# Seven block products in place of eight for the down projections of a feed-forward, with ScalarE and VectorE staggered by a step

## Chip, core and metric

The kernel runs on one core of a Trainium2 chip. Its engines are TensorE (PE: matmuls from SBUF into eight PSUM banks of 512 fp32 columns), VectorE (DVE), ScalarE (ACT), GpSimd (POOL) and SyncE (SP), which here only issues transfers. The metric is the device time of one execution in microseconds (us); lower is better.

## What is computed

Two blocks follow each other on 256 tokens of width 1024. The first has two layers of three kinds of attention, each with a gated feed-forward; the second has a mixer of four branches and a feed-forward with a squared ReLU. The change concerns only that last feed-forward:

```python
u = rms_norm(h, norm_mlp_pre[l])
hid = jnp.square(jax.nn.relu(jnp.einsum("btd,df->btf", u, w_up[l])))    # 1024 -> 4096
m = jnp.einsum("btf,fd->btd", hid, w_down[l])                           # 4096 -> 1024
h = h + rms_norm(m, norm_mlp_post[l])
```

All of it is fp32. The kernel gets the accuracy from two roundings: each operand is split into a high part, rounded to the type that TensorE multiplies in one pass, and a low part, the rest. A product is the sum of three matmuls: high by high, high by low, low by high.

## The kernel before

**Weights.** They come as a stream of tiles of 128 partitions by 2048 fp32 columns (1 MB), in the order of `stream_plan` (for the feed-forward: up 0, up 1, down 0, up 2, down 1, and so on). `load` (L2845 on) brings a tile into one of four `raw` slots as soon as the tile four places back has been split. ScalarE writes the high part (`whi`, L1374), then VectorE (L1895) or, for some tiles, GpSimd (L2772, in pieces of 256 columns) writes `wlo = raw - whi`. `whi` and `wlo` have three slots each (`SPL`). Each engine's program is written in order, and `ahead(...)` places the split of the tile two ahead into it. In the feed-forward of the second block both splits belong to ScalarE and VectorE; GpSimd has none.

**The feed-forward.** It runs in 16 steps. Step j computes 256 hidden features: `wide` (L735) makes two blocks of 128 features by 512 columns (256 tokens times the high and the low part of the input) in banks 0 and 1 or 2 and 3, with 8 matmuls of 512 columns each and 8 of 256 for the low part of the weights. VectorE adds the two halves of each block with a reduction that reads PSUM (`summed`, L1931) and squares the positive part in place (L2727) into `cc` or `th`; ScalarE rounds it to `gh` (L1868), and VectorE writes `gl` (L2729). `down` (L756) of step j-1 then adds 2 token halves x 2 feature blocks x 2 column halves, each three matmuls of 512 columns (L771 to L773), into the four banks 4 to 7, where they stay until the last step. `down_quarter` (L776) does the last step one bank at a time, so that the norm can begin on the first.

**Around it.** Before the stage stands the norm `post1`: ScalarE squares and sums, VectorE adds, GpSimd takes the root (`root`, L2781), VectorE multiplies by the gain and adds to the residual stream `X` (L2379, L2387), and TensorE transposes `X` (L586) for the up projection. After it stands the same with `post2`, and four transfers out.

```python
for j in range(16):                                   # tensor_program, second block
    b = 2 * (j % 2)
    if j:
        wide(tile_at[2, "up", j, 0], (b, b + 1), lp)
...
    if j:
        down(tile_at[2, "down", j - 1, 0], j - 1, False)
```

## Time and profile before

| | us |
|---|---|
| median of 3 runs | 1020.5 |
| lowest, highest | 1020.02, 1020.83 |
| span of the profiled execution | 1018.8 |

| engine | busy us | share of the span |
|---|---|---|
| TensorE | 1010.3 | 99% |
| VectorE | 758.5 | 74% |
| ScalarE | 556.8 | 55% |
| GpSimd | 232.6 | 23% |

The span is the profiled execution's own time between its first and last instruction; the runs' times include what lies around it. The stage of the change is the last sixth of the span. Matmuls overlap in the array, so the length of a single one is not its share of TensorE's time; the difference of two starts is.

### The profile page before, as it was taken

What the parts mean: (1) busy time and instruction counts of PE and PEld (TensorE: products, weight loads), DVE (VectorE), ACT (ScalarE), POOL (GpSimd) and SP (SyncE); (2) the same over time, 40 slices, a digit from 0 to 9 for tenths busy, and PEclk for the clock granted to TensorE, in tenths of its full rate; (3) what the DMA queues carried; (4) which work ended last, traced back from release to release, by engine and by line L of the source; (5) the groups of instructions that cost most, each with busy time, mean ns of one, the idle gap of its engine ahead of it and who ended that gap; (6) DMA issues with size and microseconds to landing.
All of it is one profiled execution on the core that took longest, in us unless ns stands there. A gap on an engine that the chain in (4) does not pass through costs nothing.

```text
span 1018.8 us, 14751 instructions
## 1 busy us (share of the span) xinstructions
PE 1010.3 (99%) x5688; PEld 851.1 (84%) x5688; DVE 758.5 (74%) x1208; ACT 556.8 (55%) x848; POOL 232.6 (23%) x322
## 2 busy tenths in 40 slices
PE   9999999999999999999999999999999999999997
PEld 6877788888888877788888888998888888888886
DVE  6997568788777887578787778888865457766665
ACT  6575566545556466656554556845544455334433
POOL 0572600000000272800000004019947620000000
PEclk9999999999999999999999999999999999999999
DMA  9641545555554351365554544553445556564541
GB/s 362 232 159 59 176 155 207 190 182 207 194 180 173 114 218 42 125 221 193 212 195 177 207 168 163 171 201 119 170 150 184 204 186 227 191 214 174 182 149 41
DMA packets 27894, 180.24 MB, mean 177 GB/s; under 512 B 3120, under 2 KB 3248, under 8 KB 7472
## 3 DMA queue, kind: packets, MB, share of 16 engines
q1 hardware_dynamic: 27824, 179.30, 49.5%
q8 instruction: 45, 0.74, 0.3%
q14 instruction: 25, 0.20, 0.1%
HBM read 178.24 MB, written 1.05 MB: 176 GB/s over the span
## 4 chain that ended last, share of the span: by engine, by line
PE 97%; DVE 1%; ACT 1%; DMA 0%; issue 0%; SPq 0%; DVEq 0%
PE pb L747 17%; PE pb L752 10%; PE pb L609 9%; PE pb L610 9%; PE pb L612 8%; PE pb L772 6%; PE pb L771 6%; PE pb L773 6%; PE pb L754 3%; PE pb L1017 2%; PE pb L970 2%; PE pb L673 1%; PE pb L672 1%; PE pb L674 1%; PE pb L709 1%; PE pb L985 1%
## 5 line engine op out<-in xcount | busy, mean ns | idle before, releaser
L1895 DVE TENSOR_TENSOR wlo<-raw,whi 128x2048 fp32r<-128x2048 f32 (+1 forms) x125 | 282.8, 2265 | 102.4 <-ACT whi L1374 102.2
L1374 ACT ACTIVATE whi<-raw 128x2048 fp32r<-128x2048 f32 x159 | 298.5, 1881 | 60.5 <-PE pb L612 34.6
L2772 POOL TENSOR_TENSOR wlo<-raw,whi 128x256 fp32r<-128x256 f32 x268 | 206.8, 810 | 318.9 <-ACT whi L1374 315.2
L747 PE MATMUL pb<-hb,whi 128*128 128x512 f32 x770 | 183.7, 389 | 0.0
L747 PEld LDWEIGHTS pb<-hb,whi 128*128 128x128 f32 x770 | 144.6, 188 | 30.4
L609 PE MATMUL pb<-whi,hb 128*128 128x512 f32 x336 | 134.2, 399 | 0.1
L610 PE MATMUL pb<-wlo,hb 128*128 128x512 f32 x336 | 130.9, 390 | 0.0
L612 PE MATMUL pb<-whi,hb 128*128 128x512 f32 x320 | 124.9, 390 | 0.0
L752 PEld LDWEIGHTS pb<-hb,wlo 128*128 128x128 f32 x880 | 112.8, 191 | 4.3
L752 PE MATMUL pb<-hb,wlo 128*128 128x256 f32 x880 | 114.2, 283 | 0.0
L772 PE MATMUL pb<-wlo,gh 128*128 128x512 f32 x280 | 109.2, 390 | 0.0
L773 PE MATMUL pb<-whi,gl 128*128 128x512 f32 x280 | 109.1, 390 | 0.0
L771 PE MATMUL pb<-whi,gh 128*128 128x512 f32 x280 | 109.0, 389 | 0.0
L2781 POOL TENSOR_TENSOR sm<-sm 128x1 f32<-128x1 f32 x12 | 6.5, 553 | 422.7 <-DVE sm L1903 243.3
L609 PEld LDWEIGHTS pb<-whi,hb 128*128 128x128 f32 x336 | 63.1, 188 | 14.5 <-issue 2.3
L610 PEld LDWEIGHTS pb<-wlo,hb 128*128 128x128 f32 x336 | 63.2, 188 | 12.1
L612 PEld LDWEIGHTS pb<-whi,hb 128*128 128x128 f32 x320 | 60.1, 188 | 12.8
L771 PEld LDWEIGHTS pb<-whi,gh 128*128 128x128 f32 x280 | 52.6, 188 | 11.6 <-issue 0.3
L772 PEld LDWEIGHTS pb<-wlo,gh 128*128 128x128 f32 x280 | 52.6, 188 | 11.2
L773 PEld LDWEIGHTS pb<-whi,gl 128*128 128x128 f32 x280 | 52.6, 188 | 11.0
L1538 ACT ACTIVATE gh<-th 128x512 fp32r<-128x512 f32 x22 | 13.9, 632 | 76.3 <-DVE th L2281 76.3
L754 PE MATMUL pb<-hb,whi 128*128 128x512 f32 x110 | 34.7, 397 | 0.0
(404 smaller groups left out, 1558.8 us busy)
## 6 DMA issues: line engine op xcount, KB each, us to landing
raw<-wst SPq DMA_DIRECT2D x159, 1024.0 KB, 4.8
raw<-wst SPq DMA_DIRECT2D x10, 512.0 KB, 4.3
gb<-gains SPq DMA_DIRECT2D x3, 512.0 KB, 6.4
XN<-xt SPq DMA_DIRECT2D x2, 512.0 KB, 5.3
X<-x SPq DMA_DIRECT2D x1, 1024.0 KB, 12.1
out<-X SPq DMA_DIRECT2D x4, 256.0 KB, 2.0
PQ<-prm SPq DMA_DIRECT2D x1, 909.0 KB, 4.5
raw<-wst SPq DMA_DIRECT2D x2, 256.0 KB, 7.3
```

The lines of the kernel that those rows point to most:

```text
L609: e.matmul(o, high[:, s], wh[:, k, :], start=first and k == 0, stop=False)
L610: mm = e.matmul(o, high[:, s], wl[:, k, :], start=False, stop=False)
L612: mm = e.matmul(o, low[:, s], wh[:, k, :], start=False, stop=last and k == 3)
L747: e.matmul(b[:, :], wh[:, k, s], hb2[:, k, :, :].rearrange("p i q -> p (i q)"), start=k == 0, stop=False)
L752: e.matmul(b[:, 0:L], wl[:, k, s], hh[:, k, :], start=False, stop=False)
L754: mm = e.matmul(b[:, :], wh[:, 7, s], hb2[:, 7, :, :].rearrange("p i q -> p (i q)"), start=False, stop=True)
L771: e.matmul(o, ah, wh[:, k, c], start=j == 0 and k == 0, stop=False)
L772: e.matmul(o, ah, wl[:, k, c], start=False, stop=False)
L773: mm = e.matmul(o, al, wh[:, k, c], start=False, stop=last and k == 1)
L1374: e.activation(whi[:, split_slot(m), 0:w], raw[:, m % RAW, 0:w], ACT.Copy).then_inc(*hi(m))
L1895: e.tensor_tensor(wlo[:, split_slot(m), s], raw[:, m % RAW, s], whi[:, split_slot(m), s].bitcast(F32), ALU.subtract).then_inc(*lo_v(m))
L2772: g = e.tensor_tensor(wlo[:, split_slot(m), s], raw[:, m % RAW, s], whi[:, split_slot(m), s].bitcast(F32), ALU.subtract)
```

## The change

Each step's down product is a product of 2 x 2 blocks: hidden features in two blocks by tokens in two halves (the first operand), features by column halves (the weights). The changed kernel forms it as seven block products in place of eight, in the form that uses sums of blocks: products 1, 2 and 4 take blocks of hidden features as they are, products 3, 5, 6 and 7 take sums of such blocks over the token halves (token sums); the weights are the four quarters of the down tile, one of them rewritten as a sum, and three more sums of quarters (weight sums). Each of the seven accumulates over the 16 steps in a PSUM bank of its own (banks 1 to 7), and the four blocks of the result are put together from them once, at the end. Bank 0 alone is left for the up blocks.

- **TensorE**: `wide_block` makes one up block; the products of a step are spread over two places, 3, 5, 6, 7 of step j-2 between the two up blocks of step j and 1, 2, 4 of step j-1 behind them.
- **ScalarE** copies each up block from PSUM into `E` (`evict`), rounds the token sums and the weight sums as well (`features_high`, `sums_high`), and is a step behind with `gh`.
- **VectorE** adds the halves out of `E`, forms three token sums, and writes the low halves of `gh`, of the token sums and of two of the three weight sums.
- **GpSimd** forms the three weight sums and one sum in the raw tile itself (`weight_sums`, pieces of 256 columns) and the low half of the third weight sum (`sums_low`).
- The weights of a down tile are laid out in memory as four blocks of 512 columns. The split of a down tile waits for `weight_sums`, since that changes the raw tile. Odd down tiles have their own slot (`odd_high`, `odd_low`), in memory that earlier stages used.
- At the end ScalarE copies product 1, VectorE makes four totals with seven additions, and the gain of the first column half goes to GpSimd; the second token half goes out first.

The core of the diff:

```diff
+            def quarter_products(j, *names):
+                m = downs[j]
...
+                for n in names:
+                    if n in (1, 2, 4):
+                        weights_ready(m)
+                        q.wait_ge(*gl_done[m])
+                    else:
+                        q.wait_ge(*tokens_lo[j])
+                    if n in (5, 6):
+                        q.wait_ge(*sums_lo[j])
+                    if n == 7:
+                        q.wait_ge(*sums_lo_g[j])
...
+                    e.matmul(o, high, w_high, start=j == 0, stop=False)
+                    e.matmul(o, high, w_low, start=False, stop=False)
+                    mm = e.matmul(o, low, w_high, start=False, stop=j == 15)
...
-                for j in range(16):
-                    b = 2 * (j % 2)
-                    if j:
-                        wide(tile_at[2, "up", j, 0], (b, b + 1), lp)
...
+                for j in range(1, 16):
+                    wide_block(ups[j], 0, up_bank(j, 0), lp)
+                    free[up_bank(j, 0)] = ff_low[2, j, 0]
+                    if j > 1:
+                        quarter_products(j - 2, 3, 5, 6, 7)
+                    wide_block(ups[j], 1, up_bank(j, 1), lp)
+                    free[up_bank(j, 1)] = ff_low[2, j, 1]
+                    quarter_products(j - 1, 1, 2, 4)
+                quarter_products(14, 3, 5, 6, 7)
+                quarter_products(15, 1, 2, 4, 6, 7, 5, 3)
...
+                for j in range(16):
+                    if j > 1:
+                        quarters_high(j - 1)
+                    evict(j, 0)
                     if j:
-                        ahead(2, "down", j - 1, 0)
...
+                        features_high(j - 1)
+                    if j == 15:
+                        quarters_high(15)
+                    if j:
+                        sums_high(j - 1)
+                    evict(j, 1)
+                    if j < 14:
+                        split(ups[j + 2])
...
+                pieces(o[:, 0:512], r[:, 1024:1536], r[:, 0:512], ALU.subtract).then_inc(*pool())
+                pieces(o[:, 1024:1536], r[:, 1536:2048], r[:, 1024:1536], ALU.add)
+                q.wait_ge(*q.prev)
+                pieces(o[:, 512:1024], r[:, 1536:2048], o[:, 0:512], ALU.add).then_inc(*pool())
+                q.wait_ge(*q.prev)
+                pieces(r[:, 1024:1536], o[:, 512:1024], r[:, 512:1024], ALU.subtract).then_inc(*summed_w(j))
...
+            q.wait_ge(*b_used[3, 1, 1, "sum"])
+            weight_sums(0)
             root("post1")
-            m = ahead_to(m, 2, "down", 15, 0)
-            root("post2")
+            for j in range(16):
+                if j < 15:
+                    weight_sums(j + 1)
...
+                sums_low(j)
+            for t in range(2):
+                post_gain(t)
+            root("post2", (1, 0))
```

**VectorE, one step near the end.** Before, the low halves of down tile 13 and up tile 15, then step 14 up to `gl`; `[waits ...]` names the signals that an instruction waits for (`hi`: the high half is written; `used`, `half_used`: TensorE is through with a tile or its first block).

```order
L1895 TENSOR_TENSOR wlo<-raw,whi 128x2048 [waits hi]
L1895 TENSOR_TENSOR wlo<-raw,whi 128x2048 [waits used,hi]
L1931 TENSOR_REDUCE cc<-pb 128x256 [waits half_used]
L1931 TENSOR_REDUCE cc<-pb 128x256 [waits used]
L2727 SCALAR_TENSOR_TENSOR cc<-cc 128x512 [waits ff_sum]
L2729 TENSOR_TENSOR gl<-cc,gh 128x512 [waits gh_done]
```

After, the low halves of up tile 15 and down tile 13, `gl` and the sums' low halves of step 13, then the hidden features and token sums of step 14 (`shared_low` and `odd_low` are low halves of the weight sums and of odd down tiles, `tokens_low` and `mg` low halves of token sums):

```order
L2042 TENSOR_TENSOR wlo<-raw,whi 128x2048 [waits used,hi]
L2042 TENSOR_TENSOR odd_low<-raw,odd_high 128x2048 [waits hi]
L2897 TENSOR_TENSOR gl<-th,gh 128x512 [waits gh_done]
L2900 TENSOR_TENSOR mg<-token_sums,mg 128x512 [waits tokens_hi]
L2871 TENSOR_TENSOR shared_low<-sums_51,shared_high 128x1024 [waits sums_hi]
L2880 TENSOR_TENSOR cc<-E 128x512 [waits ff_low]
L2882 SCALAR_TENSOR_TENSOR cc<-cc 128x512 [waits ff_sum]
L2888 TENSOR_TENSOR token_sums<-cc 128x256 [waits ff_glu,tokens_lo]
L2890 TENSOR_TENSOR token_sums<-token_sums,cc 128x128 [waits dve]
L2892 TENSOR_TENSOR token_sums<-token_sums,cc 128x128 [waits dve]
```

Two reductions out of PSUM have become an addition out of `E`, and four kinds of operations are new; `gl` of a step no longer follows its own hidden features but stands behind both splits of the next round.

**GpSimd, from the last low half ahead of the feed-forward.** Before:

```order
L2772 TENSOR_TENSOR wlo<-raw,whi 128x256 [waits used,hi]
L2772 TENSOR_TENSOR wlo<-raw,whi 128x256 x7
L2825 MEMSET PT 128x512 [waits mm_small]
L2781 TENSOR_TENSOR sm<-sm 128x1 [waits mean_sq] x4
```

After, to the sums of down tile 1 (`sums` are the weight sums, `sm` the norm's statistics, from which `root` takes its powers):

```order
L3076 MEMSET PT 128x512 [waits mm_small]
L3002 TENSOR_TENSOR sums_50<-raw 128x256 [waits s_raw3,b_used]
L3002 TENSOR_TENSOR sums_50<-raw 128x256 x3
L3002 TENSOR_TENSOR sums_50<-raw,sums_50 128x256 [waits pool]
L3002 TENSOR_TENSOR sums_50<-raw,sums_50 128x256
L3002 TENSOR_TENSOR raw<-sums_50,raw 128x256 [waits pool]
L3002 TENSOR_TENSOR raw<-sums_50,raw 128x256
L3032 TENSOR_TENSOR sm<-sm 128x1 [waits mean_sq] x2
L3002 TENSOR_TENSOR sums_51<-raw 128x256 [waits s_raw1]
L3002 TENSOR_TENSOR sums_51<-raw 128x256 x3
L3002 TENSOR_TENSOR sums_51<-raw,sums_51 128x256 [waits pool]
L3002 TENSOR_TENSOR sums_51<-raw,sums_51 128x256
```

The sums of the first down tile stand ahead of the norm's root now, and eight pieces for each further tile behind it, with two for a low half in each step.

**TensorE, the last up tile and the start of the products behind it.** Before:

```order
L747 MATMUL pb<-hb,whi 128x512 [waits ff_sum]
L747 MATMUL pb<-hb,whi 128x512 x6
L752 MATMUL pb<-hb,wlo 128x256 [waits lo_v]
L752 MATMUL pb<-hb,wlo 128x256 x15
L754 MATMUL pb<-hb,whi 128x512 x2
L771 MATMUL pb<-whi,gh 128x512 [waits gl_done,lo_v,hi]
L772 MATMUL pb<-wlo,gh 128x512
L773 MATMUL pb<-whi,gl 128x512
L771 MATMUL pb<-whi,gh 128x512
L772 MATMUL pb<-wlo,gh 128x512
```

After, from product 7 of step 13 over the second block of up tile 15 to product 1 of step 14:

```order
L859 MATMUL pb<-shared_high,mg 128x512 [waits sums_lo_g]
L860 MATMUL pb<-shared_low,mg 128x512
L861 MATMUL pb<-shared_high,mg 128x512
L819 MATMUL pb<-hb,whi 128x512 [waits ff_low]
L819 MATMUL pb<-hb,whi 128x512 x6
L823 MATMUL pb<-hb,wlo 128x256 x8
L824 MATMUL pb<-hb,whi 128x512
L859 MATMUL pb<-whi,gh 128x512 [waits gl_done,lo_v,hi]
L860 MATMUL pb<-wlo,gh 128x512
L861 MATMUL pb<-whi,gl 128x512
```

The second block's matmuls begin when the copy of the first has left bank 0 (`ff_low`), and behind them come products 1, 2 and 4 of the step before.

## Rows read from the trace of the kernel before

**Rows 1.** Page, part 1, whole span: busy us (share) x instructions.
```profile
PE 1010.3 (99%) x5688; PEld 851.1 (84%) x5688; DVE 758.5 (74%) x1208; ACT 556.8 (55%) x848; POOL 232.6 (23%) x322
```

**Rows 2.** Chain of waits: start us, us, engine, output, line, count.
```profile
975.06 3.17 PE pb L747 x14
978.24 1.91 PE pb L752 x16
980.15 0.47 PE pb L754 x2
986.07 3.17 PE pb L747 x14
...
997.08 3.17 PE pb L747 x14
```

**Rows 3.** VectorE's timeline, one step: start, us, operation, count [idle before].
```profile
929.91 2.29 DVE L1895 TENSOR_TENSOR wlo<-raw,whi 128x2048 fp32r<-128x2048 f32 x1 [1.11 <-ACT whi L1374]
...
936.39 1.29 DVE L1931 TENSOR_REDUCE th<-pb 128x256 f32<-128x512 f32 x2 [1.01 <-PE pb L754]
937.72 0.69 DVE L2727 SCALAR_TENSOR_TENSOR th<-th 128x512 f32<-128x512 f32 x1
```

**Rows 4.** ScalarE's timeline in the same step.
```profile
931.13 1.92 ACT L1374 ACTIVATE whi<-raw 128x2048 fp32r<-128x2048 f32 x1 [1.26 <-PE pb L773]
938.44 0.63 ACT L1868 ACTIVATE gh<-th 128x512 fp32r<-128x512 f32 x1 [5.39 <-DVE th L2727]
```

**Rows 5.** GpSimd's timeline, with the count of pieces.
```profile
347.26 5.84 POOL L2772 TENSOR_TENSOR wlo<-raw,whi 128x256 fp32r<-128x256 f32 x8 [24.95 <-ACT whi L1374]
...
797.16 3.94 POOL L2772 TENSOR_TENSOR wlo<-raw,whi 128x256 fp32r<-128x256 f32 x4 [1.69 <-ACT whi L1374]
803.49 5.61 POOL L2772 TENSOR_TENSOR wlo<-raw,whi 128x256 fp32r<-128x256 f32 x8 [2.40 <-ACT whi L1374]
812.63 7.04 POOL L2772 TENSOR_TENSOR wlo<-raw,whi 128x256 fp32r<-128x256 f32 x8 [3.52 <-ACT whi L1374]
...
831.48 0.56 POOL L2781 TENSOR_TENSOR sm<-sm 128x1 f32<-128x1 f32 x1 [11.35 <-DVE sm L1903]
...
1011.86 0.55 POOL L2781 TENSOR_TENSOR sm<-sm 128x1 f32<-128x1 f32 x1 [177.11 <-DVE sm L2738]
```

**Rows 6.** VectorE's timeline ahead of the second block's output projection.
```profile
798.59 1.21 DVE L2694 TENSOR_TENSOR PQ<-PQ 128x512 f32<-128x512 f32 x1
799.72 0.67 DVE L2688 SCALAR_TENSOR_TENSOR PQ<-PQ,pb 128x512 f32<-128x512 f32 x1
...
809.93 0.69 DVE L2694 TENSOR_TENSOR PQ<-PQ 128x512 f32<-128x512 f32 x1
...
811.90 2.29 DVE L1895 TENSOR_TENSOR wlo<-raw,whi 128x2048 fp32r<-128x2048 f32 x1
```

**Rows 7.** VectorE's timeline in the first block's second layer.
```profile
347.00 0.29 DVE L2011 TENSOR_TENSOR sc<-sc,mskt 128x128 f32<-128x128 f32 x1
...
349.44 0.83 DVE L542 TENSOR_TENSOR sm<-PQ,prmt 128x128 f32<-128x128 f32 x1
350.19 0.82 DVE L543 TENSOR_TENSOR sm<-PQ,prmt 128x128 f32<-128x128 f32 x1
```

**Rows 8.** Weight load issued at 819.7: duration ns, starts; then issue to landing.
```profile
L2852 SPq DMA_DIRECT2D raw<-wst x1: 328/328/328, 819.7 to 819.7; - x1
...
DMA to landing us min/median/max: 8.1/8.1/8.1
```

**Rows 9.** Who waited for whom from 819 to 850: total us, times, longest.
```profile
PEld pb L586 <- DVE X L2387: 0.7, 2, 0.5
```

**Rows 10.** VectorE's timeline, its last operations.
```profile
1015.35 1.41 DVE L2387 SCALAR_TENSOR_TENSOR X<-XN,sm,X 128x512 f32<-128x512 f32 x2
```

**Rows 11.** VectorE's low halves, all: duration ns min/median/max.
```profile
L1895 DVE TENSOR_TENSOR wlo<-raw,whi x125: 1237/2292/2295, 22.6 to 999.1; 128x2048 fp32r<-128x2048 f32 x122, 128x1024 fp32r<-128x1024 f32 x3
```

**Rows 12.** Stretch after the last matmul: busy us by engine, then granted TensorE clock.
```profile
1014.00:1018.80 4.80, 0.00 (x0) 0.00 (x0) 2.65 (x5) 0.25 (x2) 0.55 (x1) 0.65 0.58 219
```

More of the change, by code:

```diff
@@ L388, in stacked @@
             return whi[:, split_slot(m), 0:1024].rearrange("p (k i c) -> p k i c", k=8, i=2)
+        ups = [tile_at[2, "up", j, 0] for j in range(16)]
+        downs = [tile_at[2, "down", j, 0] for j in range(16)]
+        last_out = tile_at[2, "out", 1, 1]
+        ODD_SLOT = 3
         def split_slot(m):
+            if m in ups:
+                return nth[ups[ups.index(m) % 2]] % SPL
+            if m == downs[15]:
+                return split_slot(ups[14])
+            if m in downs:
+                return ODD_SLOT if downs.index(m) % 2 else nth[last_out] % SPL
             return nth[m] % SPL
         def slot_before(m):
+            if m in ups[2:]:
+                return ups[ups.index(m) - 2]
+            if m == downs[15]:
+                return ups[14]
+            if m in downs:
+                return downs[downs.index(m) - 2] if downs.index(m) > 1 else last_out
             return order[nth[m] - SPL] if nth[m] >= SPL else None
@@ L755, in wide, with wide_block @@
                     mm.then_inc(*(used(m) if j else half_used(m)))
+            def wide_block(m, i, bank, ready):
+                wh, wl = (w.rearrange("p (k c) -> p k c", k=8) for w in parts(m))
+                s, b = slice(128 * i, 128 * i + 128), PB[bank]
+                q.wait_ge(*hi[m])
+                bank_free(bank)
+                for k in range(7):
+                    q.wait_ge(*ready[k])
+                    e.matmul(b[:, :], wh[:, k, s], hb2[:, k, :, :].rearrange("p i q -> p (i q)"), start=k == 0, stop=False)
+                q.wait_ge(*ready[7])
+                q.wait_ge(*lo_of(m)[m])
+                for k in range(8):
+                    e.matmul(b[:, 0:L], wl[:, k, s], hh[:, k, :], start=False, stop=False)
+                mm = e.matmul(b[:, :], wh[:, 7, s], hb2[:, 7, :, :].rearrange("p i q -> p (i q)"), start=False, stop=True)
+                mm.then_inc(*(used(m) if i else half_used(m)))
@@ L1858, in second_block, with evict @@
                 high_half(n, 1, par2("lp"))
-                for j in range(16):
-                    ahead(2, "up", j, 0)
-                    if j == 0:
-                        square_half(n, 0)
-                        square_half(n, 1)
-                    z = (cc, th)[j % 2][:, :, :]
+                def evict(j, i):
+                    q.wait_ge(*(used if i or not j else half_used)[ups[j]])
+                    if j > 1:
+                        q.wait_ge(*ff_sum[2, j - 2])
+                    elif j:
+                        q.wait_ge(*squares[("lp", 2), 1, 1])
+                    e.activation(E[:, 2 * (j % 2) + i, :], PB[up_bank(j, i)][:, :], ACT.Copy).then_inc(*ff_low(2, j, i))
@@ new lines, in second_block @@
+                sums_high(15)
+                features_high(15)
+                q.wait_ge(*product[1])
+                q.wait_ge(*ff_sum[2, 15])
+                e.activation(E[:, 0, :], PB[PRODUCTB[1]][:, :], ACT.Copy).then_inc(*act("first product"))
+                for i, (t, c) in enumerate(((0, 0), (1, 0), (1, 1), (0, 1))):
+                    q.wait_ge(*total[t, c])
+                    e.activation((E[:, 2, :], E[:, 3, :], rl[:, 0, :], rl[:, 1, :])[i], total_at[t, c], ACT.Square, scale=1.0 / 32,
+                                 accum_out=norm_of["post2"][:, 2 * t + c:2 * t + c + 1]).then_inc(*squares("post2", t, c))
@@ L2713, in second_block @@
+                split(downs[0])
                 for j in range(16):
[L2714 removed]
                     if j == 1:
[L2716 to L2721 removed]
@@ L2730, in second_block @@
-                    if j:
-                        ahead(2, "down", j - 1, 0)
-                ahead(2, "down", 15, 0)
-                for t in range(2):
-                    post_gain("post2", t, 0, 48)
-                    q.wait_ge(*squares["post2", t, 1])
+                        input_scale()
+                    if 0 < j < 15:
+                        split(ups[j + 1])
+                    if j > 1:
+                        split(downs[j - 1])
+                    if j:
+                        features_low(j - 1)
@@ new lines, in second_block @@
+                    if j == 15:
+                        q.wait_ge(*hi[downs[15]])
+                        high, low = parts(downs[15])
+                        e.tensor_tensor(low[:, 0:1024], raw[:, downs[15] % RAW, 0:1024], high[:, 0:1024].bitcast(F32),
+                                        ALU.subtract).then_inc(*lo_v(downs[15]))
+                    if j:
+                        sums_low(j - 1)
+                    hidden_and_sums(j)
+                features_low(15)
+                sums_low(15)
@@ new lines, in second_block, with bank @@
+                one, up, upper, side = E[:, 0, :], sums_at[0][:, 512:1024], sums_at[0][:, 1024:1536], E[:, 1, :]
+                def bank(i):
+                    q.wait_ge(*product[i])
+                    return PB[PRODUCTB[i]][:, :]
+                q.wait_ge(*act["first product"])
+                e.tensor_tensor(total_at[0, 0], one, bank(2), ALU.add).then_inc(*total(0, 0))
+                e.tensor_tensor(up, one, bank(6), ALU.add).then_inc(*dve())
+                q.wait_ge(*q.prev)
+                e.tensor_tensor(upper, up, bank(7), ALU.subtract).then_inc(*dve())
@@ L2881, in sync_program @@
                 load(m)
-            for t in range(2):
+            for t in (1, 0):
                 for n in range(2):
```

220 lines of the change are left out of this document (175 added, 45 removed).

## The prediction

> **What bounds the kernel now.** I read the page's busy shares first, then the chain of waits through the stage of the change, then VectorE's, ScalarE's and GpSimd's timelines there. TensorE is busy for 99% of the span [rows 1], and in the stage of the change the chain is TensorE alone. One of the sixteen steps takes 986.07 - 975.06 = 11.0 us: 5.55 us for two up blocks (3.17 + 1.91 + 0.47) and 5.46 us for the 24 matmuls of a down tile, 0.2275 us each [rows 2]. The 0.39 us that a matmul has in other views is its length in the pipeline, not its share of time. In such a step VectorE works on the two low halves (2.29 each), 1.29 on the two PSUM reductions and 0.69 each on the squaring and gl, about 7.2 us with idle stretches between [rows 3]; ScalarE works 1.92 us on each of two high halves and 0.63 on gh, 4.4 us together [rows 4]; GpSimd does nothing for 177 us before 1011.86 [rows 5]. So anything taken from TensorE counts, until another engine needs more than TensorE does.
>
> **What TensorE saves.** Seven products of three matmuls replace eight: 21 for 24. That is 3 x 0.2275 = 0.68 us a step, 10.9 us over 16 steps, and the step that TensorE asks for is 10.33 us. Nothing else on TensorE changes in size.
>
> **What the others get.** What counts is the distance from one start to the next: a row's length less 0.09 us where operations are independent (two reductions of 0.69 take 1.29), and plus 0.03 where the next waits for it [rows 3]. That gives 2.19 us for 2048 columns, 0.60 or 0.72 for 512, and by the slope between them 1.12 for 1024, 0.45 for 256 and 0.32 or 0.20 for 128.
> ScalarE adds per step two evictions (0.60 each), one more 512-column rounding and 1536 columns of rounded sums (about 1.4): 4.4 + 3.3 = 7.7 us. It fits into 10.33.
> VectorE keeps the two low halves (4.38), does gl and the new low half of the token sums (1.20), 1024 columns of the sums' low halves (1.12), the addition out of E and the squaring (1.44), and three token sums (0.98): 9.1 us in ten operations. Alone it would fit too, with 1.2 us to spare.
> GpSimd gets ten pieces of 256 columns per step, eight for the weight sums and two for a low half, at 0.70 us a piece when nothing disturbs it (5.61 for eight) [rows 5]: 7.0 us. Alone it fits.
>
> **But VectorE and GpSimd don't run alone.** The same 512-column addition of two SBUF operands (L2694) takes 0.69 us while GpSimd is idle (809.93) and 1.21 us while GpSimd works (798.59, between pieces that began at 797.16) [rows 5, 6]: it waits 0.53 us for a piece to end. Operations in a row on 128 columns, 0.29 us with GpSimd idle (347.00), come out at 0.83 us while eight pieces run (347.26), and their pitch of 0.75 us is 0.13 us of columns plus 0.62 for a piece [rows 5, 7]. The other way round, eight pieces that begin inside a 2048-column subtraction take 7.04 us instead of 5.61; the extra 1.4 us is what was left of that subtraction (811.90 + 2.29 = 814.19) [rows 5, 6]. L2688, which has one operand in PSUM, keeps its 0.67 us beside the pieces [rows 6]. So the two engines exclude each other when both VectorE operands lie in SBUF, whichever is first.
> Today that is harmless: GpSimd is idle in this stage, and each reduction reads PSUM. After the change all ten VectorE operations have two SBUF operands (the up results come through E now), and GpSimd always has pieces waiting. The two take turns: 9.1 us plus ten waits of 0.53, less 0.1 us in each of the dependent ones, where the piece starts in the gap that was there anyway, is 14.0 to 14.4 us. By the port's own time: 7680 columns at 1.04 ns (2.29 - 0.69 us for 1536 columns) are 8.0 us, ten pieces at 0.62 are 6.2, together 14.2. I take **14.2 us a step**. Who has priority doesn't matter to this sum. TensorE, at 10.33, waits some 3.8 us in each step for gl of the tile before its products 1, 2 and 4.
> The Trainium skill weighs in here: its page "SBUF — State Buffer", section "Who interferes with whom", says that a VectorE instruction with two SBUF inputs and a GpSimd instruction that reads SBUF contend for a port pair, and that whoever is first holds it for the whole instruction. The rows agree on the exclusion (1.21 against 0.69 us). They show a little less than the whole instruction, since by that reading a step would be 9.1 + 7.0 = 16.1 us and the total about 1103 us; that is a rival below.
>
> **The edges.** Here I went through the five engines' lists in their new order by hand, each operation starting when its engine, its signals and, on VectorE and GpSimd, the shared port are free, with the durations above and weight loads landing in time, as they do now. GpSimd now does the weight sums of tile 0 ahead of the root for the norm in front of the stage. Tile 0 is issued at 819.7 and lands 8.1 us later, at 827.8 [rows 8]; eight pieces and two waits between them end at 833.6, and the root ran at 831.48 [rows 5]. That is 2.1 us late, on the path, since TensorE already waits for the residual updates behind it, 0.7 us in all [rows 9]. The second token half's updates and the low half of up tile 1 meet pieces of tile 1's sums, 3 x 0.53. Together +3.7 us before up tile 1.
> Steps 1 and 2: GpSimd still idles between its jobs, TensorE has no or few products to do, and by the same count the two take 22.1 us against 22.0: +0.1.
> Steps 3 to 14: 12 x (14.2 - 11.0) = +38.
> The end, from the start of up tile 15 to the last residual update: before, 997.08 to 1016.76, 19.7 us [rows 2, 10]. After, VectorE begins step 14's addition 0.6 us later, needs 15.6 us to step 15's (no up tile to split, but 3.4 us of waiting for ScalarE, which waits for GpSimd's last sums), 8.6 us for that step and its low halves, and 8.8 us for seven combinations (0.6 or 0.72 each), the gains, the root (0.55) and four updates (0.6 each): 33.6 us, +13.9.
> The gain of 10.9 us is inside these step times, not added. Sum: 3.7 + 0.1 + 38 + 13.9 = +55.7. The profiled span is 1018.8 us, and its run's time is 1.7 us more than the span, as the median of 1020.5 has it: 1020.5 + 55.7 = **1076 us**.
>
> **Bounds of the unknown.** No low half of 2048 columns in the trace ever began behind a piece (the longest of all took 2.295 us) [rows 11], so its wait is not shown. At zero for both of them a step is 13.1 us and the total 1076 - 14 x 1.1 = 1061; at a whole pitch of 0.70 us for all ten it is 15.0 and 1087. I take 0.53 since all 128 to 512-column cases agree on it.
>
> **Rivals.** (1) *The exclusion bites one way only*: VectorE waits for about half of its operations, and a waiting piece still slips through. 9.1 + 5 x 0.53 = 11.8 us a step, 14 x 2.4 less: 1043. Against it: the 7.04 us [rows 5]. (2) *No exclusion here*, as if these tiles didn't meet: TensorE sets the pace. -10.9, +3.7 at the start, +2.1 of waits for gl in the first and last step, +2.4 for the longer combination behind the last matmul (the four additions that depend on each other, then the gains): -2.7, 1018 us. This is the case on the other side; it decides if VectorE's step stays below 10.33 us, for which its ten waits together would have to stay below 1.2 us. (3) *Whole instructions exclude*, 16.1 us a step: 1103. (4) *TensorE's clock falls in the new gaps.* After TensorE's last matmul the granted clock of the last 4.8 us averages 0.65 [rows 12], so with TensorE idle it fell to the lower level, 1.2 GHz, and the new waits leave TensorE idle too. At half clock the 10.33 us of a step stretch into the wait that is there anyway; only if nearly all of it ran so would a step be 20.7 us and the total near 1165. A slower TensorE also removes the gap that slows it, so I expect a lower clock on the page and no more time. The Trainium skill, page "TensorE: Matmul & The Clock Gate", section "Why this matters for your kernels", warns of idle gaps between bursts of matmuls for this reason; the row agrees as to the direction.
>
> **Chances.** Forecast, 1061 to 1087: 0.72. (1) 0.10, (2) 0.07, (3) 0.07, (4) 0.04. The range takes in the forecast's bounds and (1): 1042 to 1090. Three runs of this kernel tell about 0.2%, 2 us, from no change; (2) lies just beyond that, so of its 0.07 I count 0.04 as faster and 0.03 as same. All the rest is slower, 0.93.
>
> **What would show it.** Right: TensorE 10 or 12 points less busy in the second block's last stretch, its waits put down to VectorE's gl or the low halves; VectorE near 100% there, 512-column operations at 1.2 us and 2048-column ones at 2.8; GpSimd pieces whose mean is well above 0.7; steps of 14.2 us. Wrong: 512-column operations at 0.69 us beside working GpSimd, or steps of 10.3 us. The start is wrong if the root's operation of the norm ahead of the stage still starts by 831.5 us.

## The result, and the profile after

The changed kernel takes **1076.0 us** (median of 4 runs, 1075.6 to 1078.4) against 1020.5 us before (4 runs, 1020.0 to 1020.8): a ratio of 1.055, 95% interval 1.054 to 1.057. It is 55.6 us slower. The span of the profiled execution grew from 1018.8 to 1074.5 us, by 55.7.

The page of the changed kernel, part 1 (busy us, share, instructions), the slices of TensorE and of its granted clock, and the chain's shares by engine:
```profile
PE 1022.6 (95%) x5638; PEld 855.0 (80%) x5640; DVE 862.9 (80%) x1277; ACT 605.8 (56%) x913; POOL 446.1 (42%) x490
...
PE   9999999999999999999999999999999887888794
...
PEclk9999999999999999999999999999999898998987
...
PE 75%; DVE 15%; POOL 3%; issue 3%; DMA 2%; ACT 1%; SPq 0%; DVEq 0%; POOLq 0%; ACTq 0%
```
Against [rows 1], TensorE went from 99% to 95% of a longer span although its program has 48 matmuls fewer (the count of weight loads; of the matmul records two more are missing), VectorE did 104 us more, and GpSimd's busy time nearly doubled. TensorE's slices fall from 9 to 8 and 7 exactly where the stage of the change begins. Its busy time rises, since a matmul counts longer when it runs at the lower clock.

VectorE's timeline for one step (start us, us, engine, line, operation, count), where [rows 3] show the step before:
```profile
927.01 0.77 DVE L2888 TENSOR_TENSOR token_sums<-cc 128x256 f32<-128x256 f32 x1
927.81 0.71 DVE L2890 TENSOR_TENSOR token_sums<-token_sums,cc 128x128 f32<-128x128 f32 x1
928.56 0.71 DVE L2892 TENSOR_TENSOR token_sums<-token_sums,cc 128x128 f32<-128x128 f32 x1
929.20 5.56 DVE L2042 TENSOR_TENSOR wlo<-raw,whi 128x2048 fp32r<-128x2048 f32 x2
934.68 1.21 DVE L2897 TENSOR_TENSOR gl<-cc,gh 128x512 fp32r<-128x512 f32 x1
...
938.62 1.22 DVE L2880 TENSOR_TENSOR th<-E 128x512 f32<-128x512 f32 x1
...
941.20 0.78 DVE L2888 TENSOR_TENSOR token_sums<-th 128x256 f32<-128x256 f32 x1
```
From one L2888 to the next are 14.19 us, with no idle time in a bracket. The 512-column operations take 1.21 us, not 0.69, and the two of 2048 columns 5.56, not the 4.48 that two take undisturbed (shown below). GpSimd's timeline in the same step:
```profile
925.54 3.58 POOL L3002 TENSOR_TENSOR sums<-raw 128x256 f32<-128x256 f32 x4 [0.33 <-DMA raw<-wst]
929.08 3.52 POOL L3002 TENSOR_TENSOR sums<-raw,sums 128x256 f32<-128x256 f32 x2
932.68 3.79 POOL L3002 TENSOR_TENSOR raw<-sums,raw 128x256 f32<-128x256 f32 x2
936.43 2.86 POOL L3016 TENSOR_TENSOR shared_low<-sums,shared_high 128x256 fp32r<-128x256 f32 x2
939.82 1.87 POOL L3002 TENSOR_TENSOR sums<-raw 128x256 f32<-128x256 f32 x2 [0.53 <-DMA raw<-wst]
```
Ten pieces last 13.75 us, 1.4 us each, twice the 0.70 us of a piece alone [rows 5]. Both engines are full, and each spends a good part of that time waiting for the other: about half of it on GpSimd, about a third on VectorE. What TensorE waited for between 850 and 1060 us (waiter, releaser: total us, times, longest):
```profile
PE pb L859 <- DVE gl L2897: 35.9, 14, 3.7
PE pb L859 <- DVE shared_low L2871: 2.6, 1, 2.6
```
So it waits for `gl` in 14 places, 2.6 us in the mean; the rest of what a step has too much goes into matmuls at the lower clock.

### The profile page after: what moved, and what is told of

It reads as the page before. It is cut to its first block, busy times and chain, and to the rows that moved or that the text cites. A ratio compares the mean times of both kernels' runs of the same rounds, so it can differ in the third digit from the quotient of the medians.

```text
span 1074.5 us, 14968 instructions
## 1 busy us (share of the span) xinstructions
PE 1022.6 (95%) x5638; PEld 855.0 (80%) x5640; DVE 862.9 (80%) x1277; ACT 605.8 (56%) x913; POOL 446.1 (42%) x490
## 4 chain that ended last, share of the span: by engine, by line
PE 75%; DVE 15%; POOL 3%; issue 3%; DMA 2%; ACT 1%; SPq 0%; DVEq 0%; POOLq 0%; ACTq 0%
PE pb L801 12%; PE pb L663 8%; PE pb L664 7%; PE pb L666 7%; PE pb L806 7%; DVE wlo L2042 4%; PE pb L882 3%; PE pb L883 3%; PE pb L881 3%; PE pb L808 2%; POOL sums L3002 2%; PE pb L1127 2%; PE pb L1080 2%; DVE shared_low L2871 2%; DMA raw<-wst 2%
## 5 line engine op out<-in xcount | busy, mean ns | idle before, releaser
L1485 ACT ACTIVATE whi<-raw 128x2048 fp32r<-128x2048 f32 x143 | 268.0, 1878 | 43.8 <-PE pb L666 34.6
L801 PE MATMUL pb<-hb,whi 128*128 128x512 f32 x560 | 133.7, 389 | 0.0
L801 PEld LDWEIGHTS pb<-hb,whi 128*128 128x128 f32 x560 | 105.1, 188 | 22.2
L806 PEld LDWEIGHTS pb<-hb,wlo 128*128 128x128 f32 x640 | 82.1, 191 | 3.1
L806 PE MATMUL pb<-hb,wlo 128*128 128x256 f32 x640 | 83.0, 283 | 0.0
L882 PE MATMUL pb<-wlo,gh 128*128 128x512 f32 x160 | 62.4, 390 | 0.0
L883 PE MATMUL pb<-whi,gl 128*128 128x512 f32 x160 | 62.3, 389 | 0.0
L881 PE MATMUL pb<-whi,gh 128*128 128x512 f32 x160 | 62.3, 389 | 0.0
L3002 POOL TENSOR_TENSOR sums<-raw 128x256 f32<-128x256 f32 x64 | 56.5, 911 | 13.8 <-DMA raw<-wst 11.8
L819 PE MATMUL pb<-hb,whi 128*128 128x512 f32 x210 | 57.4, 416 | 0.0
L1649 ACT ACTIVATE gh<-th 128x512 fp32r<-128x512 f32 x22 | 13.9, 632 | 76.3 <-DVE th L2427 76.3
L3002 POOL TENSOR_TENSOR raw<-sums,raw 128x256 f32<-128x256 f32 x32 | 54.4, 1719 | 1.3
## 6 DMA issues: line engine op xcount, KB each, us to landing
X<-x SPq DMA_DIRECT2D x1, 1024.0 KB, 12.2
```

What stands on the lines that cost most here:

```text
L801: e.matmul(b[:, :], wh[:, k, s], hb2[:, k, :, :].rearrange("p i q -> p (i q)"), start=k == 0, stop=False)
L806: e.matmul(b[:, 0:L], wl[:, k, s], hh[:, k, :], start=False, stop=False)
L881: e.matmul(o, ah, wh[:, k, c], start=j == 0 and k == 0, stop=False)
L882: e.matmul(o, ah, wl[:, k, c], start=False, stop=False)
L883: mm = e.matmul(o, al, wh[:, k, c], start=False, stop=last and k == 1)
L1485: e.activation(parts(m)[0][:, 0:w], raw[:, m % RAW, 0:w], ACT.Copy).then_inc(*hi(m))
```

## The experiments

Times are medians, but for two kernels that ran once, where the text says so. Each experiment was run beside the kernel before on the same chip, and ratios are against it. "A step" is the mean distance of the hidden addition (L2880) from step 1 to step 15, if nothing else is said.

**Take the reads away, keep everything else.** Rival (2) and the forecast differ only in whether GpSimd's pieces disturb VectorE. So the pieces become writes without a source.
```diff
-                        g = e.tensor_tensor(dst[:, c:c + PIECE], a[:, c:c + PIECE], b[:, c:c + PIECE], op)
+                        g = e.memset(dst[:, c:c + PIECE], 0.0)
```


> GpSimd's ten pieces per step in the feed-forward are replaced by memsets of the same columns: it writes and signals as before but reads nothing, so the weight sums are wrong and the output isn't the reference's. Nothing else differs from the changed kernel. Theory (VectorE and GpSimd exclude each other when both read SBUF with two operands on VectorE): VectorE's 512-column operations go back from 1.22 to 0.69 us and the 2048-column ones from 2.83 to 2.29, a step is TensorE's 10.3 us, and the total is 1015 to 1021 us. Rival (VectorE's or ScalarE's amount of work sets the pace whatever GpSimd does): 1060 us or more. Rival (half of the waits come from elsewhere): about 1043 us.

Measured: 1017.1 us, ratio 0.997 (0.996 to 0.998), a step of 10.4 us. VectorE's timeline, then a row of GpSimd's:
```profile
925.77 0.69 DVE L2880 TENSOR_TENSOR cc<-E 128x512 f32<-128x512 f32 x1 [0.72 <-ACT E L1977]
...
928.29 4.48 DVE L2042 TENSOR_TENSOR wlo<-raw,whi 128x2048 fp32r<-128x2048 f32 x2
...
936.12 0.69 DVE L2880 TENSOR_TENSOR th<-E 128x512 f32<-128x512 f32 x1 [0.73 <-ACT E L1977]
```
```profile
927.43 1.58 POOL L3002 MEMSET sums<- 128x256 f32 x6 [3.01 <-DMA raw<-wst]
```
The same operations are back at 0.69 and 4.48 us, VectorE idles again, and the step is what TensorE asks for (10.33 by the prediction). So nothing but the pieces makes the change slow. The writes are also shorter (0.26 us each), but that isn't what helps: in the steps of the changed kernel VectorE never stands idle, so what decides is how long its own operations take. The run also bounds the idea: if the sums cost VectorE nothing, the whole gain would be 3 us.

**Fewer pieces.** The second piece of each pair in the weight sums, four a step, becomes such a write.
```diff
+                        if c:
+                            g = e.memset(dst[:, c:c + PIECE], 0.0)
+                        else:
+                            g = e.tensor_tensor(dst[:, c:c + PIECE], a[:, c:c + PIECE], b[:, c:c + PIECE], op)
```

> Every second piece of the weight sums is a memset, so four of the ten pieces per step read nothing; half of the sums' columns are wrong and the output isn't the reference's. Theory: the step is the sum of what both engines hold, 8.0 us of VectorE columns and 0.62 us for each reading piece: 8.0 + 6 x 0.62 = 11.7 us, 2.5 us less in each of some 14 steps, so about 1041 us (1036 to 1047). Rival (a threshold: any contention costs all of it): stays near 1076 us. Rival (GpSimd's own chain of work sets the pace, its pieces being slow): the memsets are shorter than pieces but still count, about 1055 us.

Measured: 1046.5 us in a single run, just inside the range, and a step of 12.2 us where 11.7 were expected. Six pieces give 12.20 and ten give 14.16: 0.49 us a piece, close to the 0.53 us that one wait takes.

**No pieces, their work on VectorE.** The weight sums and the whole low half of the sums (1536 columns) are VectorE's:
```diff
+                    e.tensor_tensor(o[:, 0:512], r[:, 1024:1536], r[:, 0:512], ALU.subtract).then_inc(*dve())
+                    e.tensor_tensor(o[:, 1024:1536], r[:, 1536:2048], r[:, 1024:1536], ALU.add)
...
+                    if 0 < j < 15:
+                        weight_sums(j + 1)
                     hidden_and_sums(j)
```


> VectorE does all of GpSimd's feed-forward pieces itself: four additions of 512 columns per step and 1536 columns of the sums' low half in place of 1024; GpSimd does nothing in the stage but its last tile's part and the roots. Same results, same other engines. Theory: nobody to wait for, VectorE needs 9.1 + 2.6 + 0.5 = 12.2 us a step, 2.0 us less than together with GpSimd, total about 1047 us (1040 to 1054), although VectorE has more work than in the changed kernel. Rival (VectorE is simply overloaded, its operations long for a reason of their own): 14.2 + 3.2 = 17.4 us a step, near 1120 us.

Measured: 1078.9 us in a single run, a miss by 32 us. VectorE's waits (850 to 1060) and its timeline:
```profile
DVE sums L2878 <- DMA raw<-wst: 24.5, 12, 2.2
```
```profile
932.09 0.69 DVE L2878 TENSOR_TENSOR sums<-raw 128x512 f32<-128x512 f32 x1 [2.09 <-DMA raw<-wst]
...
946.56 0.69 DVE L2878 TENSOR_TENSOR sums<-raw 128x512 f32<-128x512 f32 x1 [2.05 <-DMA raw<-wst]
```
Every operation has its undisturbed length, but this step is 14.47 us, of which VectorE stands 2.05 for a load. A load is issued when the tile four places back has been split, and this order asked for its data too early. I had not looked at where the load lands. The next kernel moves the sums behind the hidden values of the step:
```diff
-                    if 0 < j < 15:
-                        weight_sums(j + 1)
                     hidden_and_sums(j)
+                    if 0 < j < 15:
+                        weight_sums(j + 1)
```


> As sums_on_vector (all of the weights' sums and their low part on VectorE, nothing on GpSimd in the feed-forward of the second block), with one edit: VectorE forms the sums of step j+1 behind the gate and the sums of the hidden columns of step j, not ahead of them. In sums_on_vector VectorE stood 12 times, 24.5 us in all, for the load that the sums read, and took 14.46 us a step. Theory (the miss of sums_on_vector was this wait for a load and nothing else): the load has landed by the time that VectorE comes to the sums, the step falls to VectorE's own work of 12.4 us, and the time to 1078.9 - 24.5 = about 1054, range 1050 to 1058. Rival (the wait hid one for something else, a buffer or ScalarE, that now comes up): the step stays over 13.5 us and the time over 1068.

Measured: 1053.1 us, ratio 1.032 (1.031 to 1.034), a step of 12.4 us in the mean and 12.32 in the middle of the stage, no wait for a load. Two hidden additions on VectorE's timeline (L2891 in that kernel):
```profile
933.36 0.68 DVE L2891 TENSOR_TENSOR th<-E 128x512 f32<-128x512 f32 x1
...
945.68 0.69 DVE L2891 TENSOR_TENSOR cc<-E 128x512 f32<-128x512 f32 x1
```
In this kernel the four additions take 2.53 us (923.55 to 926.08), and the low half of 1536 columns 1.75 us where that of 1024 takes 1.23. So the same elements cost VectorE 3.1 us a step when it does them itself. Without them its step would be 12.32 less 3.05, that is 9.3 us, so when GpSimd does them beside it, they cost it 14.2 - 9.3 = 4.9 us. This is the fastest form of the change that computes the reference, and it is still slower than before: VectorE's own work is more than TensorE's 10.33 us.

**The other direction: pieces into the kernel before.** Ten pieces of 256 columns that read and write unused columns, in each step:
```diff
+            for j in range(16):
+                q.wait_ge(*ff_glu[2, j])
+                for i in range(10):
+                    e.tensor_tensor(PQ[:, 2200 + 300 * i:2456 + 300 * i], PQ[:, 5600:5856], PQ[:, 6000:6256], ALU.add).then_inc(*pool())
+                q.wait_ge(*q.prev)
```


> The kernel before, with ten added GpSimd pieces of 256 columns in each of the 16 feed-forward steps, two SBUF operands each, results unused. Theory: VectorE's operations with two SBUF operands grow by up to 0.53 us each (2.29 to 2.83, 0.69 to 1.22), at most four of them a step, so VectorE needs 7.2 + 2.1 = 9.3 us of the 11.0 that TensorE takes, and the time stays at 1020.5 us within 2. Rival (every wait at the port is paid in full): 4 x 0.53 x 16 = +34 us, 1054 us.

Measured: 1041.0 us, between the two expectations. VectorE's timeline, then GpSimd's at the end:
```profile
925.47 1.29 DVE L1931 TENSOR_REDUCE cc<-pb 128x256 f32<-128x512 f32 x2 [0.78 <-PE pb L754]
926.79 1.25 DVE L2727 SCALAR_TENSOR_TENSOR cc<-cc 128x512 f32<-128x512 f32 x1
...
936.48 1.29 DVE L1931 TENSOR_REDUCE th<-pb 128x256 f32<-128x512 f32 x2 [0.40 <-PE pb L754]
```
```profile
1004.02 28.64 POOL L2831 TENSOR_TENSOR PQ<-PQ 128x256 f32<-128x256 f32 x40
1032.74 0.55 POOL L2781 TENSOR_TENSOR sm<-sm 128x1 f32<-128x1 f32 x1
```
The steps stayed at 11.01 us, and the reductions, which read PSUM, at 1.29 for two. The time went behind the stage: ten disturbed pieces take more than a step, and a queue of them stood ahead of the last root, which began at 1032.74 instead of 1011.86 [rows 5]. That was a fault of the experiment. With six pieces in place of ten:

> The kernel before, with six added GpSimd pieces of 256 columns in each step of the feed-forward of the second block instead of the ten of before_with_pieces; they read and write columns that nothing uses. Ten of them took GpSimd 12.45 us where a step lasts 11.0, so a backlog of pieces stood ahead of the last square root. Six take about 7.5 us and leave no backlog. Theory (before, VectorE has idle time in which it makes up what the pieces make it wait, and TensorE sets the step; all 20 us of before_with_pieces were the backlog): 1020.5, range 1019.5 to 1022.5, steps of 11.0 us. Rival (part of the 20 us was VectorE's waiting, in the steps or in the run-out): six tenths of 20.6, about 1033.

Measured: 1020.7 us, ratio 1.0006 (0.9997 to 1.0015). GpSimd is busy or waiting for 8.78 of each 11.0 us and the kernel doesn't notice:
```profile
928.24 8.78 POOL L2831 TENSOR_TENSOR PQ<-PQ 128x256 f32<-128x256 f32 x6 [2.22 <-DVE cc L2727]
939.25 8.79 POOL L2831 TENSOR_TENSOR PQ<-PQ 128x256 f32<-128x256 f32 x6 [2.23 <-DVE th L2727]
```
VectorE's two-operand operations do get longer here, but within its idle time. The pieces alone are not the price. The price is pieces beside a VectorE with 1.2 us to spare.

**What is paid for: instructions or columns?** Three kernels change the pieces of the changed kernel. Five of 512 columns:
```diff
-                    for c in range(0, 512, PIECE):
-                        g = e.tensor_tensor(dst[:, c:c + PIECE], a[:, c:c + PIECE], b[:, c:c + PIECE], op)
+                    for c in range(0, 512, 512):
+                        g = e.tensor_tensor(dst[:, c:c + 512], a[:, c:c + 512], b[:, c:c + 512], op)
```
and likewise in `sums_low`; twenty of 128, by the same edit with 128; and four more of 256, in `sums_low`:
```diff
+                for again in range(3):
+                    if again:
+                        g.then_inc(*pool())
+                        q.wait_ge(*q.prev)
+                    for c in range(1024, 1536, PIECE):
```

> The changed kernel with each pair of GpSimd pieces of 256 columns in the weights' sums as one operation of 512 columns: five operations a step for ten, the same elements. It asks what VectorE pays for: a fixed price for each GpSimd instruction, or the time for which its columns pass. Theory (by the columns; a piece of 256 columns makes VectorE wait 0.53 us, one of 512 some 1.1): the step stays 14.2 us, the time 1075, range 1068 to 1083. Rival (a fixed price of 0.53 us an instruction): 5 x 0.53 = 2.7 us less a step, 11.6 us, about 12 x 2.6 + 3 less, 1042, range 1038 to 1048.

> The changed kernel with each GpSimd piece of 256 columns in the weights' sums as two of 128: twenty a step for ten, the same elements. With pieces of 512 the time was 1077.8. Theory (VectorE pays for the columns, whatever the piece; ten pieces of 256 make it wait 5.1 us a step): the step stays 14.2 us, up to 0.5 more for the gaps between more instructions, time 1076 to 1084. Rival (each VectorE operation waits for one piece at most, of which a shorter one costs half, and it has about eleven operations a step: 11 x 0.27 = 3.0 us): 12.1 us a step, about 1048, range 1044 to 1054.

> The changed kernel with four more GpSimd pieces of 256 columns a step: the two of the low part of the sums are done three times over, each pair behind the pair before, to the same values. Ten pieces keep GpSimd busy or waiting for 13.7 of the 14.2 us of a step, 1.37 us a piece. Theory (VectorE is what the step waits for, and each piece costs it 0.53 us): 16.3 us a step, 16 x 2.1 = 34 us more, 1110, range 1100 to 1118. Rival (GpSimd has no time left, each of its pieces waits out a VectorE operation, and it becomes the bound at 14 x 1.37 = 19.2 us a step): 16 x 5.0 = 80 us more, 1156, range 1135 to 1165.

Measured: 1077.8, 1099.8 and 1122.4 us, steps of 14.4, 15.8 and 17.1 us. The stretch from 870 to 1010 us in the changed kernel, then with pieces of 512, of 128, and with four more (columns: window, its length, busy us and count of PE, PEld, DVE, ACT and POOL, granted TensorE clock, DMA share, GB/s):
```profile
870.00:1010.00 140.00, 114.44 (x524) 94.33 (x523) 137.96 (x100) 74.23 (x71) 135.41 (x99) 0.91 0.39 146
```
```profile
870.00:1010.00 140.00, 113.91 (x523) 93.98 (x522) 138.07 (x96) 71.76 (x70) 99.79 (x50) 0.92 0.37 140
```
```profile
870.00:1010.00 140.00, 111.64 (x467) 90.74 (x466) 97.71 (x90) 65.02 (x63) 137.85 (x175) 0.85 0.35 134
```
```profile
870.00:1010.00 140.00, 101.62 (x449) 83.22 (x447) 111.25 (x87) 59.67 (x57) 136.77 (x115) 0.87 0.34 129
```
With 512 columns the fixed price for each instruction is refuted: half the instructions, and VectorE is as full as before (138.1 of 140). One of its operations there:
```profile
927.01 1.67 DVE L2882 SCALAR_TENSOR_TENSOR cc<-cc 128x512 f32<-128x512 f32 x1
```
It takes 0.98 us more than the undisturbed 0.69: fewer waits, each about twice as long. With 128 both of my expectations miss. VectorE's share fell to 97.7 us, and GpSimd is the full one. A row of VectorE's timeline and two of GpSimd's in that kernel tell why:
```profile
940.77 0.94 DVE L2897 TENSOR_TENSOR gl<-cc,gh 128x512 fp32r<-128x512 f32 x1
```
```profile
934.73 1.69 POOL L3002 TENSOR_TENSOR raw<-sums,raw 128x128 f32<-128x128 f32 x4
...
938.25 7.32 POOL L3002 TENSOR_TENSOR sums<-raw 128x128 f32<-128x128 f32 x8 [0.17 <-POOL shared_low L3016]
```
A VectorE operation waits for one piece, now 0.26 us (0.94 less 0.68), as the rival had it. But while VectorE works, a piece also waits for a VectorE operation to end: 0.92 us a piece (7.32 for eight) where it takes 0.42 alone (1.69 for four, VectorE idle). ScalarE's high half waits for GpSimd's sums, and VectorE's low half for ScalarE. Four more pieces end the same way: GpSimd full at 17.1 / 14 = 1.22 us a piece, and the time between my 1110 and 1156, outside both ranges. All of this fits one reading: the engines **take turns by instruction**, and each waits for at most the one instruction that the other is in. With about as many VectorE operations as pieces in a step both wait about once each, and both are full; with more pieces GpSimd becomes the bound.

**The start.** The sums of step 0 stand ahead of the norm's root on GpSimd. One kernel puts the root first:
```diff
-            weight_sums(0)
             root("post1")
+            weight_sums(0)
```


> The changed kernel with one edit: GpSimd takes the square root of post1 ahead of the sums of step 0's weights, as the kernel before has nothing in its way there. In the changed kernel that root runs at 832.46 instead of 831.48 us. Theory (the start lost 0.9 us to the sums ahead of the root, and this is the only price there): the second block's feed-forward starts 0.8 to 1.0 us earlier; the sums of step 0 come 1 us later, and nothing waits for them, since their products come in step 2. Time 1075.1, range 1074.5 to 1075.8. Rival (VectorE's chain, not the start, carries the time, and the later pieces fall on VectorE's norm and gate instead): 1076, unchanged.

Measured: 1079.9 us (5 runs, 1079.7 to 1080.7), 3.9 us slower than the changed kernel, against both expectations. ScalarE's timeline, then VectorE's:
```profile
843.84 1.92 ACT L1982 ACTIVATE whi<-raw 128x2048 fp32r<-128x2048 f32 x1 [3.90 <-POOL raw L3002]
```
```profile
849.27 0.69 DVE L2880 TENSOR_TENSOR cc<-E 128x512 f32<-128x512 f32 x1 [1.19 <-ACT E L1977]
```
"Nothing waits for them" was wrong: the high half of down tile 0 waits for these sums, and the evictions of up tile 0 stand behind it on ScalarE. The hidden addition moved from 846.00 to 849.27. The sums themselves now ran beside VectorE's work and ended 11 us later. The next kernel also takes that high half behind the evictions, and its low half on VectorE behind the hidden values of step 0:
```diff
-                quarters_high(0)
                 square_half(n, 0)
...
                     evict(j, 1)
+                    if j == 0:
+                        quarters_high(0)
```


> As root_before_first_sums, with a second edit: ScalarE rounds the weights of step 0's down projection behind the evictions of up tile 0, not ahead of the squares of the input, and VectorE forms their low part behind the gate of step 0. In root_before_first_sums that rounding stood first on ScalarE and waited 3.90 us for GpSimd's sums, which came later than with the sums ahead of the root (the last one ended at 843.8, not 832.5), and the squares and the evictions of up tile 0 stood behind it; the time rose by 3.8 us. Theory (the rise was this queue on ScalarE and nothing else, and the root's delay itself costs 0.9 us): the evictions of tile 0 come no later than in the changed kernel, and the time is 1075.1, range 1073.5 to 1076. Rival (the rise came from GpSimd's pieces meeting VectorE's work of the first step): still over 1078.

Measured: 1078.9 us (5 runs), the rival's number. VectorE's timeline (its lines are one higher there), then TensorE's:
```profile
844.53 0.70 DVE L2881 TENSOR_TENSOR cc<-E 128x512 f32<-128x512 f32 x1 [1.84 <-ACT E L1977]
...
848.69 2.28 DVE L2043 TENSOR_TENSOR wlo<-raw,whi 128x2048 fp32r<-128x2048 f32 x1
...
852.25 2.83 DVE L2043 TENSOR_TENSOR wlo<-raw,whi 128x2048 fp32r<-128x2048 f32 x1
855.00 1.21 DVE L2898 TENSOR_TENSOR gl<-cc,gh 128x512 fp32r<-128x512 f32 x1
```
```profile
856.36 0.77 PE L859 MATMUL pb<-whi,gh 128*128 128x512 f32 x1 [7.49 <-DVE gl L2898]
856.92 0.63 PE L860 MATMUL pb<-wlo,gh 128*128 128x512 f32 x1
857.35 0.63 PE L861 MATMUL pb<-whi,gl 128*128 128x512 f32 x1
```
The hidden addition came 1.5 us earlier, so the queue on ScalarE was real. But gl(0) begins at 855.0 instead of 850.98, so 5.5 us came in between, and TensorE waits 7.5 us for gl. Of these, 2.2 us are a low half that now stands between the hidden values and gl; in the changed kernel VectorE writes it in time that it would mostly have spent waiting for the copy, like the 1.84 us here. The other 3.3 us are waits for GpSimd's pieces, above all those of tile 1's sums, which ended at 841.7 in the changed kernel and here run beside step 0's operations until 852.2: an addition of 128 columns takes 0.71 us there, not 0.29, and the four small operations on the statistics 1.4 us together, not 0.3. So the rival's cause is in the trace as well. The root ran 1.0 us earlier in this kernel (831.42), yet up tile 1 began only 0.5 us earlier (843.14 instead of 843.64), since the norm's second token half waits for the last bank of the projection ahead of it. I found no order in which the root's 1.0 us comes back, and tried only these two.

## Why the prediction was right, point by point

- **What TensorE saves** (0.68 us a step, 10.33 left): right. With pieces that read nothing a step is 10.4 us.
- **The exclusion**, 0.53 us a wait: right, and taken from a place in the kernel before where the engines met for a few microseconds. 512-column operations at 1.21 us [rows 6], steps of 14.2.
- **The unknown**, whether a 2048-column operation waits too: it does, like the rest. 5.56 less 4.48 us is 0.54 for each of the two. The lower bound of 1061 falls. The upper bound was mis-summed: "a whole pitch of 0.70 us for all ten" is 9.1 + 7.0 = 16.1 us, as in rival (3); its 15.0 is the 8.0 us of columns plus 7.0. Nothing hung on it.
- **"Who has priority doesn't matter"**: right for ten against ten only. My sum by the port's columns gives nearly the same step whatever the size of a piece, and fails with pieces of 128 (15.8 us). What gave 14.2 was one wait for each VectorE operation.
- **Steps 3 to 14**: predicted +38, measured +38.6. TensorE begins up tile 3 at 867.70 and up tile 15 at 1038.35, 14.22 us a step; before, at 864.84 and 996.91, 11.01 us a step. The prediction's 997.08 for the last is the chain's time, which counts from the end of the matmul before. After, then before:
```profile
1038.35 2.27 PE L819 MATMUL pb<-hb,whi 128*128 128x512 f32 x7
```
```profile
996.91 3.34 PE L747 MATMUL pb<-hb,whi 128*128 128x512 f32 x14
```
- **The start**: predicted +3.7, measured +1.0 (up tile 1 at 843.64 instead of 842.68). The failed term is the landing of down tile 0: I gave it the 8.1 us of [rows 8], and it landed 6.9 us after its issue at 819.7, so that its first piece began at 826.78. Why this load was quicker is not shown. GpSimd's timeline:
```profile
826.78 2.82 POOL L3002 TENSOR_TENSOR sums<-raw 128x256 f32<-128x256 f32 x4 [6.68 <-DMA raw<-wst]
...
832.46 0.55 POOL L3032 TENSOR_TENSOR sm<-sm 128x1 f32<-128x1 f32 x1
```
  So the root was 1.0 us late, not 2.1, and the later meetings with pieces fell into time that was free.
- **Steps 1 and 2**: predicted +0.1, measured +1.9 (24.06 us for 22.16). The failed step is "GpSimd still idles between its jobs": its pieces run without a break from 854.60 on, each VectorE operation from 855.10 on waits for one, and gl of step 1 begins only at 863.99. TensorE itself didn't wait for that one. It had waited 3.0 us for gl of step 0, the nine matmuls behind that wait ran at half clock (852.34 to 856.32, granted 0.50) and so did a part of the up block after them, 3.0 us more than at full clock, and it came to its products at 865.64, 0.4 us after gl was done. So all but some 0.3 us of what the clock cost there took the place of a wait for gl of step 1 that would have come anyway.
- **The end**: predicted +13.9, measured +13.6 (1038.35 to 1071.83, 33.5 us, against 996.91 to 1016.76, 19.9 us). This term is right by offsetting errors. VectorE began step 14's addition 0.65 us before up tile 15 (1037.70), not 0.6 behind it; to step 15's addition it took 14.9 us, not 15.6, with 2.6 us of waiting and not 3.4; that step took 8.6 us, as forecast; but the combinations, gains, root and updates took 10.7 us, not 8.8.
- **The sum**: 1.0 + 1.9 + 38.6 + 13.6 = 55.1 us, and 0.6 us more behind the last residual update, where the four transfers out take 2.6 us to land instead of 2.0. The span grew by the 55.7 us of the forecast. The mechanism and the large term are right; that the total is right to a tenth is luck, since the start and the end were 3.0 us too long together, and steps 1 and 2, steps 3 to 14 and the transfers 3.0 us too short.
- **Rivals.** (2) is what the kernel does without pieces: 1018 worked out, 1017.1 measured, again not term by term, since the short writes don't delay the root (831.80) as its +3.7 had it. (1) would be a step of 11.8; six pieces already make it 12.2. (3) says 16.1 us a step, measured 14.2. The Trainium skill's page "SBUF — State Buffer", section "Who interferes with whom", has the exclusion last for the whole instruction. The turns by whole instructions are what the kernels with pieces of 128 show; but the wait is 0.53 us and not the 0.70 us pitch of a piece, and for 128-column operations that depend on each other 0.42 us (0.29 to 0.71). Why an instruction shuts the other engine out for less than its own time is not shown.
- (4) **The clock** did fall in the gaps: to between 0.80 and 1.00 in stretches of 14 us, 0.91 on average from 870 to 1010 us. TensorE's busy share in that stretch is 82% after 100%, 18 points less where I had named 10 or 12. In the steps the lower clock costs nothing, as forecast: VectorE, for which TensorE waits, has no idle time there. At the end it does cost time. TensorE's timeline:
```profile
1058.85 0.39 PE L860 MATMUL pb<-wlo,gh 128*128 128x512 f32 x1
...
1060.95 0.63 PE L861 MATMUL pb<-whi,gl 128*128 128x512 f32 x1
1061.38 0.75 PE L859 MATMUL pb<-odd_high,mg 128*128 128x512 f32 x1
```
  The last two start 0.43 us apart instead of 0.23. The first, right behind a wait of 1.9 us, still ran at full clock: the level fell only while TensorE was at work again, with the matmul at 1059.78. VectorE's combinations wait for TensorE 1.2 and 0.3 us. These 1.5 us, for which my end term had no place, are most of the 1.9 us by which its last part was too short.

## What to carry to other kernels

Before work goes to an idle engine, look at what it shares with the engine that will be busiest: find a place in the profile where the two already meet and read the longer length of the same operation there. Count the turns: while both have work, a VectorE operation with two SBUF operands waits for one GpSimd instruction, and a GpSimd instruction for one of VectorE's, so work moved to GpSimd can cost VectorE more than doing it itself (4.9 against 3.1 us a step here), while beside a VectorE with idle time six such pieces a step cost the kernel nothing. When an operation is moved to an earlier or a later place in an in-order queue, check when its data land and what stands behind it; four of the expectations here went wrong at just that.

## What the runs showed of the hardware that I had not expected

- Smaller GpSimd pieces are worse, not gentler: the same columns in twenty pieces cost 24 us more than in ten, since each piece that meets VectorE's work waits for an operation of VectorE to end.
- Writes without a source (1.58 us for six of 256 columns) leave VectorE's operations at their undisturbed length.
- That TensorE's clock would fall was forecast, but not that the matmuls behind a wait would run at the lower level where they count. After the 7.5 us wait above, matmuls of 512 columns started 0.43 us apart, the lower of the two levels (1.2 against 2.4 GHz).
